# Expert layer of a two-layer decoder trunk on one Trainium2 core: tokens dispatched and combined through row tables in HBM

## What is computed

```python
for l in range(DEPTH):
    h = rms_norm(x, mix_norm_g[l])
    z = h @ w_in[l]
    y_a = gmlp_branch(...) @ gm_w_proj[l]        # chunked spatial gating
    y_b = mla_branch(...) @ mla_w_proj[l]        # latent attention, 16 heads
    gates = sigmoid(z[..., OFF_GATE:])
    x = x + (gates[0] * y_a + gates[1] * y_b) @ w_out[l]
    h2 = rms_norm(x, ffn_norm_g[l])
    if l % 2 == 0:
        x = x + swiglu(h2, dense_w_gu[l // 2], dense_w_down[l // 2])
    else:
        x = x + moe_swiglu(h2, w_router, b_router, w_gu, w_down)

def moe_swiglu(h, w_router, b_router, w_gu, w_down):
    logits = h @ w_router + b_router
    top_vals, top_idx = lax.top_k(logits, 2)
    wts = softmax(top_vals)
    combine = sum(one_hot(top_idx, 8) * wts[..., None], axis=1)
    for e in range(8):
        g, u = split(h @ w_gu[e], 2)
        y = y + combine[:, e:e + 1] * ((silu(g) * u) @ w_down[e])
    return y
```

## Time and profile before

| | us |
|---|---|
| median of 3 runs (1614.69 to 1618.01) | 1615.21 |
| profiled execution, span | 1615.1 |
| TensorE busy | 1525.3 (94%) |
| VectorE busy | 1213.4 (75%) |
| ScalarE busy | 980.7 (61%) |
| GpSimd busy | 18.8 (1%) |

### The profile page before, as it was taken

The page is one execution under the profiler, slowest core; times in us unless marked ns, Lnnn a source line. Parts: engine busy times, 40 slices in busy tenths (PEclk is TensorE's granted clock), DMA queues, the critical chain, the costliest instruction groups (busy, mean ns, idle before and its releaser), DMA issues.

```text
span 1615.1 us, 20864 instructions
## 1 busy us (share of the span) xinstructions
PE 1525.3 (94%) x7137; PEld 1238.9 (77%) x7137; DVE 1213.4 (75%) x1359; ACT 980.7 (61%) x1191; POOL 18.8 (1%) x23
## 2 busy tenths in 40 slices
PE   5998899999997998999699999999999999999996
PEld 4777777788786777778588888888888888888884
DVE  3697555656445697456698998989989899898995
...
GB/s 241 136 229 145 90 105 171 172 186 179 138 199 130 167 211 108 101 130 199 79 353 313 349 346 338 349 334 348 349 337 350 335 348 345 335 350 336 348 348 130
DMA packets 287980, 394.07 MB, mean 244 GB/s; under 512 B 13340, under 2 KB 218328, under 8 KB 287912
## 3 DMA queue, kind: packets, MB, share of 16 engines
...
q0 software_dynamic: 1184, 3.38, 0.8%
...
HBM read 392.07 MB, written 1.05 MB: 243 GB/s over the span
## 4 chain that ended last, share of the span: by engine, by line
PE 80%; DVE 10%; ACT 6%; issue 2%; DMA 1%; SPq 0%; DVEq 0%; ACTq 0%
PE ps L453 24%; PE ps L455 23%; PE ps L454 23%; DVE w_lo L430 4%; ACT w_hi L425 3%; PE ps L853 1%; PE ps L636 1%; PE ps L835 1%; PE ps L833 1%; PE ps L762 1%; PE ps L744 1%; DMA raw<-in_w_in 1%; PE ps L843 1%; PE ps L845 1%; ACT prob L1073 0%
## 5 line engine op out<-in xcount | busy, mean ns | idle before, releaser
L430 DVE TENSOR_TENSOR w_lo<-raw,w_hi 128x2048 fp32r<-128x2048 f32 (+1 forms) x306 | 645.3, 2115 | 218.6 <-ACT w_hi L425 215.3
L425 ACT ACTIVATE w_hi<-raw 128x2048 fp32r<-128x2048 f32 (+1 forms) x306 | 544.6, 1781 | 296.9 <-PE ps L455 293.7
L453 PE MATMUL ps<-w_hi,act_hi 128*128 128x512 f32 (+1 forms) x1264 | 505.1, 400 | 6.2 <-DVE w_lo L430 6.2
L455 PE MATMUL ps<-w_lo,act_hi 128*128 128x512 f32 (+1 forms) x1264 | 494.0, 391 | 0.0
L454 PE MATMUL ps<-w_hi,act_lo 128*128 128x512 f32 (+1 forms) x1264 | 492.8, 390 | 0.0
L453 PEld LDWEIGHTS ps<-w_hi,act_hi 128*128 128x128 f32 x1264 | 239.8, 190 | 53.6 <-issue 7.4
L455 PEld LDWEIGHTS ps<-w_lo,act_hi 128*128 128x128 f32 x1264 | 239.1, 189 | 51.4
L454 PEld LDWEIGHTS ps<-w_hi,act_lo 128*128 128x128 f32 x1264 | 240.1, 190 | 46.4
L430 DVE TENSOR_TENSOR w_lo<-raw_more,w_hi 128x2048 fp32r<-128x2048 f32 x96 | 202.4, 2108 | 20.7 <-ACT w_hi L425 19.7
L425 ACT ACTIVATE w_hi<-raw_more 128x2048 fp32r<-128x2048 f32 x96 | 170.6, 1777 | 69.2 <-PE ps L455 69.2
L453 PE MATMUL ps<-w_hi,ehid_hi 128*128 128x512 f32 x352 | 145.2, 413 | 1.4 <-DVE w_lo L430 0.7
...
## 6 DMA issues: line engine op xcount, KB each, us to landing
raw<-in_moe_w_gu SPq DMA_DIRECT2D x256, 512.0 KB, 8.0
raw_more<-in_moe_w_gu SPq DMA_DIRECT2D x96, 512.0 KB, 8.1
raw<-in_w_in SPq DMA_DIRECT2D x72, 512.0 KB, 4.6
raw_more<-in_moe_w_down SPq DMA_DIRECT2D x64, 512.0 KB, 6.4
raw<-in_moe_w_down SPq DMA_DIRECT2D x64, 512.0 KB, 4.9
raw<-in_dense_w_gu SPq DMA_DIRECT2D x44, 512.0 KB, 4.7
...
raw<-in_gm_w_proj SPq DMA_DIRECT2D x16, 512.0 KB, 4.3
```

The costliest lines, as they stand in the source:

```text
L425: nc.scalar.activation(w_hi[:, self.split_slot(j), 0:n], self.raw(j)[:, 0:n], ACT.Copy).then_inc(self.hi, 1)
L430: nc.vector.tensor_tensor(w_lo[:, c, 0:n], self.raw(j)[:, 0:n], w_hi[:, c, 0:n].bitcast(F32), ALU.subtract).then_inc(self.lo, 1)
L453: nc.tensor.matmul(dst, a_hi, b_hi, start=start, stop=False)
L455: return nc.tensor.matmul(dst, a_hi, b_lo, start=False, stop=stop)
```

## The change

- Token rows go through HBM. `x_rows` and `y_rows` hold 256 rows of 1024 floats for each expert. Once, in layer 0, POOL's queue fills `x_rows` and half of `y_rows` with zeros. After the router, VectorE forms the normed tokens with the gain (`xn`) and for each token and choice a row number, and POOL issues four indirect DMAs that write tokens to their rows. For each expert SP loads 128 rows into `xs`; TensorE transposes them (eight transposes in place of 32 products), ScalarE and VectorE split them without a scale.
- y is copied to `y_sb` by ScalarE and stored to `y_rows` by a DMA from ScalarE's queue. After the last expert SP signals POOL, POOL issues four indirect DMAs that read each token's two rows, VectorE adds them to `xres` with the weights `rt`, and SP stores the output in four parts. `pick`, `put`, `slot_w`, `y_hi`, `y_lo`, `xn_hi`, `xn_lo` and `combine` are gone.
- Gate/up strips are 512 columns wide: five strips of four chunks (two k tiles each, gate and up in banks of their own) and one of 256 with two chunks. Hidden turns: five of four transposes and one of two. The number of chunks and weight matmuls stays. y accumulates in banks 6 and 7, turns use 4 and 5.
- Nine raw slots in the expert part.
- In SBUF, `act_hi` and `act_lo` come first, then the mixers' transposed operands, `vbuf` and `qk_t`, over which `ehid_hi`, `ehid_lo`, two raw slots, `ehid`, `esig` and the dense layer's `hid_hi`, `hid_lo` lie, up to 61 KiB; then `w_hi` (61 to 85), `w_lo` (85 to 109), `raw` (109 to 141), and the rest.

The diff, cut to its core (blank lines left out):

```diff
-RAW, RAW_MOE, SPLIT, LEAD = 4, 6, 3, 3
+RAW, RAW_MOE, SPLIT, LEAD = 4, 9, 3, 3
...
-    GU_CHUNKS = GUS * KD // 4
+    EG_STRIPS = [STRIP] * (FF // STRIP) + [FF % STRIP] * (FF % STRIP > 0)
+    EGS = len(EG_STRIPS)
+    EG_CHUNKS = [(j, k0, CHUNK // (2 * w), w) for j, w in enumerate(EG_STRIPS) for k0 in range(0, KD, CHUNK // (2 * w))]
+    STRIP_END = [max(c for c, x in enumerate(EG_CHUNKS) if x[0] == j) + 1 for j in range(EGS)]
+    GU_CHUNKS = len(EG_CHUNKS)
...
+        j, k0, n, w = EG_CHUNKS[c]
+        v = w_gu.rearrange("(k p) n -> p k n", p=P)
+        return [v[:, k0:k0 + n, hh * FF + j * STRIP:hh * FF + j * STRIP + w] for hh in range(2)]
...
-        raw = sb("raw", [P, RAW, CHUNK])
+        act_hi = sb("act_hi", [P, KD, S], F32R)
+        act_lo = sb("act_lo", [P, KD, S], F32R)
...
+        t1_hi = sb("t1_hi", [P, KD, S], F32R, mixer)
+        t1_lo = sb("t1_lo", [P, KD, S], F32R, mixer)
+        bt_hi = sb("bt_hi", [P, KD, S], F32R, mixer)
+        bt_lo = sb("bt_lo", [P, KD, S], F32R, mixer)
...
+        ehid_hi = sb("ehid_hi", [P, KF, P], F32R, experts)
+        ehid_lo = sb("ehid_lo", [P, KF, P], F32R, experts)
+        raw_low = sb("raw_low", [P, 2, CHUNK], F32, experts)
...
+        experts.close()
+        hid_hi = sb("hid_hi", [P, KF, S], F32R)
+        hid_lo = sb("hid_lo", [P, KF, S], F32R)
         w_hi = sb("w_hi", [P, SPLIT, CHUNK], F32R)
         w_lo = sb("w_lo", [P, SPLIT, CHUNK], F32R)
-        act_hi = sb("act_hi", [P, KD, S], F32R)
-        act_lo = sb("act_lo", [P, KD, S], F32R)
+        raw = sb("raw", [P, RAW, CHUNK])
...
-        hid_hi = sb("hid_hi", [P, KF, S], F32R, ffn)
...
+        moe_slots = ([raw[:, (N0 + i) % RAW, :] for i in range(RAW)] + [raw_low[:, i, :] for i in range(2)]
+                     + [raw_more[:, i, :] for i in range(RAW_MOE - RAW - 2)])
...
+            def rows_load(q, e):
+                z = pass_sems[q]
+                if not is_first(e):
+                    sp.wait_ge(z["eturn_done"], gather_turn_no(e - 1, 1) + 1)
+                sp.dma_start(xs[:], x_rows[e, q]).then_inc(z["xs_landed"], 16)
+            def expert_loads(r, q, e, last):
+                for c in range(GU_CHUNKS):
+                    _, _, n, w = EG_CHUNKS[c]
+                    v = r.raw_view(c, n, 2 * w)
+                    g, u = expert_gu_pieces(moe_w_gu[0, e], c)
+                    r.load(sp, e, c, [(v[:, :, 0:w], g), (v[:, :, w:2 * w], u)])
+                    if q == 0 and is_first(e) and c == RAW_MOE + LEAD - 1:
+                        sp.wait_ge(rows_written, 16 * 2 * TT)
+                        rows_load(q, 0)
+                    if not last and c == GU_CHUNKS - 1:
...
             sp.wait_ge(counts_ready, 1)
             crowded = sp.value_load(most[0:1, 0:1], min_val=0, max_val=S)
...
+            sp.wait_ge(pass_sems[0]["y_stored"], 16 * E)
...
+            sp.nop().then_inc(passes_over, 1)
+            for i, (t, hf) in enumerate(TAIL):
+                sp.wait_ge(x_added, 2 * L + i + 1)
+                sp.dma_start(out[0, t * P:(t + 1) * P, hf * 512:(hf + 1) * 512],
+                             xres[:, t, hf * 512:(hf + 1) * 512]).then_inc(out_stored, 16)
...
+                    pool.wait_ge(merged_b, 2)
+                    zeros = ws_raw[:].rearrange("p g t -> p (g t)")
+                    nc.gpsimd.memset(zeros, 0.0).then_inc(zeroed, 1)
+                    pool.wait_ge(zeroed, 1)
+                    for e in range(E):
+                        pool.dma_start(x_rows[e].rearrange("s p d -> p s d"),
+                                       zeros.rearrange("p (o d) -> p o d", o=1).to_broadcast([P, 2, D])
+                                       ).then_inc(rows_zeroed, 16)
+                        pool.dma_start(y_rows[e, 1], zeros).then_inc(rows_zeroed, 16)
...
-            pool.wait_ge(xn_hi_done, 1)
-            nc.gpsimd.tensor_tensor(xn_lo[:], xn[:], xn_hi[:].bitcast(F32), ALU.subtract).then_inc(xn_lo_done, 1)
...
+            pool.wait_ge(rows_ready, 1)
+            for c in range(2):
+                for t in range(TT):
+                    pool.indirect_dma_start(x_row_list, bass.IndirectOffsetOnAxis(ap=row_i[:, c, t:t + 1], axis=0),
+                                            xn[:, t, :], None).then_inc(rows_written, 16)
+            pool.wait_ge(rows_written, 16 * 2 * TT)
+            pool.wait_ge(passes_over, 1)
+            for t in range(TT):
+                for c in range(2):
+                    pool.indirect_dma_start(raw[:, 0:2, :].rearrange("p a (b d) -> p (a b) d", d=D)[:, 2 * t + c, :], None,
+                                            y_row_list, bass.IndirectOffsetOnAxis(ap=row_i[:, c, t:t + 1], axis=0)
+                                            ).then_inc(picked[2 * t + c], 16)
...
+                def gather(e, half):
                     for k in range(4):
                         c = (4 * half + k) * P
-                        for t in range(TT):
-                            nc.tensor.matmul(bank[:, k * P:(k + 1) * P], xn_hi[:, t, c:c + P], pick[:, t, :],
-                                             start=t == 0, stop=False)
-                            mm = nc.tensor.matmul(bank[:, k * P:(k + 1) * P], xn_lo[:, t, c:c + P], pick[:, t, :],
-                                                  start=False, stop=t == TT - 1)
-                    mm.then_inc(z["g_done"], 1)
...
-                def scatter(t, g_read):
-                    for hf in range(2):
-                        pe.wait_ge(z[f"g_free{hf}"], g_read)
-                        nc.tensor.matmul(ps[:, 6 + hf, :], put[:, t * P:(t + 1) * P], y_hi[:, hf * 512:(hf + 1) * 512],
-                                         start=True, stop=False)
-                        nc.tensor.matmul(ps[:, 6 + hf, :], put[:, t * P:(t + 1) * P], y_lo[:, hf * 512:(hf + 1) * 512],
...
-                                         start=False, stop=True).then_inc(z["g_done"], 1)
+                        mm = nc.tensor.transpose(ps[:, 4 + half, k * P:(k + 1) * P], xs[:, c:c + P], ident)
...
-                    for k in range(2):
-                        mm = nc.tensor.transpose(ps[:, 4 + j % 2, k * P:(k + 1) * P], hid[:, j % 2, 0, k * P:(k + 1) * P], ident)
-                    mm.then_inc(z["hturn_done"], 1)
+                    pe.wait_ge(z[f"eturn_free{j % 2}"], turns_read(e, 2 + j))
+                    for k in range(EG_STRIPS[j] // P):
+                        mm = nc.tensor.transpose(ps[:, 4 + j % 2, k * P:(k + 1) * P], ehid[:, k * P:(k + 1) * P], ident)
+                    mm.then_inc(z["eturn_done"], 1)
...
+                    for c, (j, k0, n, w) in enumerate(EG_CHUNKS):
...
+                            pe.wait_ge(z[f"eturn_free{k0 // 4}"], turns_read(e, k0 // 4) + 1)
...
-                                hidden_turn(e, j - 2)
-                        if not first and j == 1:
-                            pe.wait_ge(z["y_split"], e)
-                            scatter(0, g_read(e, 0))
-                        if not first and j == 3:
-                            scatter(1, g_read(e, 2))
-                        if j == 5:
-                            pe.wait_ge(z["g_free0"], g_read(e, 4))
-                            for t in range(TT):
-                                mm = nc.tensor.transpose(ps[:, 6, t * P:(t + 1) * P], pick[:, t, :].bitcast(F32), ident)
-                            mm.then_inc(z["g_done"], 1)
-                            pe.wait_ge(z["g_free1"], g_read(e, 4))
-                            for t in range(TT):
-                                mm = nc.tensor.matmul(ps[:, 7, 0:1], pick[:, t, :].bitcast(F32), pick_w[:, t:t + 1],
-                                                      start=t == 0, stop=t == TT - 1)
-                            mm.then_inc(z["g_done"], 1)
+                            else:
+                                for hh in range(2):
+                                    at = slice((2 * k + hh) * w, (2 * k + hh + 1) * w)
+                                    mm = three(ps[:, b + hh, 0:w], act_hi[:, kk, 0:P], act_lo[:, kk, 0:P], ch[:, at],
+                                               cl[:, at], kk == 0, kk == KD - 1)
+                        mm.then_inc(r.used, 1)
+                        if 1 <= j < EGS - 1 and c == STRIP_END[j] - 2:
+                            hidden_turn(e, j - 1)
...
+                            pe.wait_ge(z["y_copied"], e)
...
-                            hidden_turn(e, GUS - 2)
...
+                pe.wait_ge(z["xs_landed"], 16)
+                gather(None, 0)
+                gather(None, 1)
...
-                pe.wait_ge(z["y_split"], E)
-                scatter(0, g_read(E, 0) - 1)
-                scatter(1, g_read(E, 2) - 1)
...
-            act.wait_ge(normed0_done, normed_before(L))
-            act.wait_ge(normed1_done, normed_before(L))
-            copy(xn_hi[:], xn[:]).then_inc(xn_hi_done, 1)
...
-                    act.wait_ge(z["g_free1"], g_read(e, 4) + 1)
```

(43 more changed lines are left out.)

316 lines of the change are left out of this document (135 added, 181 removed).

## The result

The changed kernel takes 1589.65 us (median of 4 runs, 1587.24 to 1591.39) against 1615.62 (4 runs, 1614.69 to 1618.01) of the kernel before on the same chip: ratio 0.9833, 95% interval 0.9819 to 0.9847, so 1.5 to 1.8% faster. The forecast was 1577 us, with a range of 1560 to 1600. The profiled execution has a span of 1587.6 us against 1615.1, so 27.5 are to be explained where 37.7 were forecast.

The account below looks back on a forecast made before the run. TensorE was taken to bound the expert stage. TensorE's work -41.5, SBUF order -9.7, zero fill +0.5, head +5 and tail +8 sum to -37.7 us, from 1615 to 1577 us, range 1560 to 1600.

Parts of the forecast that it names:

- The bound: Expert stage: it goes at TensorE's pace, so work leaving its queue leaves the time; an expert falls from 100.8 to 95.0 us.
- TensorE's work: Experts: scatter, pick and slot_w gone, cheaper gathers and hidden turns save 5.78 us per middle expert, 41.5 us together.
- Splits: Expert weight chunks: the 15.6 us of TensorE waits for low parts stay; nothing counted for the wide gate/up strips.
- The rival with a wait of 0.3 us in each of 40 wide strips: Gate/up strips: VectorE or the split chain becomes the bound, costing 12 us, 1589 us in all; chance 0.14.
- The order of SBUF: Weight matmuls: a low place makes stationary operands quicker, saving 9.7 us, with ends of -13 and +9.
- The zero fill: Layer 0, POOL's queue writing 12.6 MB of zeros at half rate beside the loads: costs 0.5 us, ends 0 and 8.
- Four ring slots of 5.4 us each cover a slower landing: Zero fill in layer 0: loaded-ahead weight slots hide slower loads, so only 0.5 us is counted.
- The head: Router to the experts' first weight matmul: row writes by indirect DMA and their landing add 5 us, from 0 to +14.
- The tail: Last expert to the end: storing y, indirect gathers, adds and output store add 8 us, from +2 to +16.
- memory at its mean rate: Expert stage: 343 GB/s is all memory gives, an expert stays at 100.8 us, 1623 us in all; chance 0.03.
- indirect DMAs row by row: Head and tail: 128 rows go one behind the other, 22 us instead of 4 per DMA, 1724 us; chance 0.06.
- gate/up staying at 346: Expert loads: wider rows stay at 346 GB/s, loads set the pace at 97.6 us per expert, 1600 us; chance 0.13.

Follow-up runs that it names:

- experiment 12: Changed kernel with each 512-column gate/up load issued as two 256-column DMAs (1 KiB rows), other loads cut in two by partitions: 1761.75 us, ratio 1.0915.
- the first profile: Profile of the changed kernel's first measurement, before it was run again unchanged on another chip: span 1587.6 us.

## Why the prediction was right, and where its numbers were not

- **The bound** was right: TensorE sets the pace, and work taken out of its queue shortens each expert. 95.2 us were measured where the sum had 95.0, or 94.5 with its share for the order of SBUF.
- **TensorE's work.** Scatter, `pick` and `slot_w` are gone as counted. A group of four transposes was mis-sized: 0.36 forecast, 0.44 measured, for gathers and hidden turns alike. So the gathers save 2.7 (not 2.86) and the turns nothing (5 x 0.44 + 0.22 = 2.42 as before, not 2.02), together 0.56 less per expert: 37.2 in the stage instead of 41.5.
- **Splits.** "I count nothing for it" was short by some 3.4 us. In starts of neighbouring weight matmuls over 0.262 us apart, less 0.23 each and without those behind a transpose, TensorE lost 8.6 us before and 11.9 after in the stretches of the waits above. The rival with a wait of 0.3 us in each of 40 wide strips did not happen: of the 23.2 us only 2.7 lie among gate/up matmuls, seven waits, each some 8.4 us behind the start of an expert and none at the end of a strip. The rest lies among the down matmuls, as before.
- **The order of SBUF.** The sign was right by luck, since the reason fell. The 0.0071 us saved on 888 mixer and dense-down matmuls are 6.3, as forecast (6.1); on `ehid` 0.0052 x 1056 = 5.5 where 3.6 stood. Both come from the distance between the two operands and not from the place: the two rows compared had differed in place and in distance, and place was the one that the diff named. On `act` in the experts 0.0015 x 2112 = 3.2 where 0 stood; the distance did not change there, and experiment 12 points at the loads' rows.
- **The expert stage** closes with these: 37.2 from the queue, 5.5 + 3.2 from the spacing, less 3.4 of waits, are 42.5 against 42.1 measured.
- **The zero fill** was mis-sized: 0.5 forecast, 1 to 2 measured in its stretch, 4 in the first profile. "Four ring slots of 5.4 us each cover a slower landing" failed because the sixteen DMAs do not run at half rate beside the loads; they are issued in one burst, and a split waited 10.7 us for its load.
- **The head**: +8.6 for +5. The issues took 6.7 us (forecast 6, as one of 2.9 and three of 1.26), the landing 5.9 (forecast 4.0, from a plain load of the earlier trace rows), and the rest is 0.9 us from the row numbers to the first issue and transposes at half clock (granted clock 0.50 from 800 to 804 us).
- **The tail**: +6.1 for +8. The gathers were issued in 4.7 us and not in 6. The branch was priced at 2.7 and cost 2.5.
- **The rivals**: memory at its mean rate fell (377 GB/s), indirect DMAs row by row fell (about 6 us each to land), gate/up staying at 346 fell (388).
- **The number.** 1577 for 1589.7 lies inside the range, but the sum is made of misses both ways: less saved on transposes, waits and a longer head against more saved on the spacing.
